# Where the low half of the feed-forward input lies in SBUF

## The chip, the cores and the metric

The kernel runs on one NeuronCore of a Trainium2 chip. The metric is the device time of one execution in microseconds (us). TensorE (PE) multiplies, VectorE (DVE) and ScalarE (ACT) work element by element, GpSimd (POOL) takes a few small roots, and SyncE (SP) issues the transfers. SBUF is the on-chip memory: an offset below is a byte offset within each of its 128 partitions. PSUM holds TensorE's results.

## The reference

Two transformer stacks run one after the other on 256 tokens of width 1024. The first has four layers; each is feed-forward, mixer, feed-forward, each with a norm before and after:

```python
def swiglu(x, w_in, w_out):
    gate, up = jnp.split(x @ w_in, 2, axis=-1)      # w_in 1024 x 5632
    return (jax.nn.silu(gate) * up) @ w_out          # w_out 2816 x 1024

for layer in range(4):
    h = h + 0.5 * rmsnorm(swiglu(rmsnorm(h, g[0]), ffn_w_in[layer, 0], ffn_w_out[layer, 0]), g[1])
    h = h + rmsnorm(mixer(rmsnorm(h, g[2])), g[3])   # sliding window, GLA, RWKV-7, sliding window
    h = h + 0.5 * rmsnorm(swiglu(rmsnorm(h, g[4]), ffn_w_in[layer, 1], ffn_w_out[layer, 1]), g[5])
```

The second stack has two layers (latent attention, neighbourhood attention) on latent and context tokens, each with a gated feed-forward block with a short convolution. Everything is float32.

## The kernel before

Every engine's instructions are written out by hand in one order for the whole program; nothing is scheduled later. Each engine waits on counting semaphores for named events.

TensorE multiplies in the format float32r, which keeps fewer bits than float32. So each operand is split in two: a high half, rounded to float32r (ScalarE, lines 708 and 886), and a low half, the rest (VectorE, lines 716 and 892). A product then takes three matmuls, issued by `mm3` on lines 186, 187 and 188: high by high, high by low, low by high. In this text a *triple* is one such group. Each matmul has its own load of 128 x 128 weights (the stationary side, PEld in the profile) and streams the other operand (256 or 512 columns).

There are feed-forward blocks numbered 0 to 8 and 10. Blocks 0 to 7 and 10 work on 256 tokens and get their memory from `ffn_memory`; block 8 works on 512 tokens (latent and context) and has memory of its own. In `pe_core`, a block of 256 tokens makes 22 steps, one for each 128 of the 2816 hidden columns. A step multiplies the input by 128 gate columns and 128 up columns: 2 x 8 triples, 48 matmuls of 256 columns, in which pieces of the weights are stationary and the input's halves `xh`, `xl` stream. Then it multiplies the hidden values of the step before by the output weights: four triples, 12 matmuls of 512 columns, in which the halves of the hidden values (`hs`) are stationary and pieces of the output weights stream. The first step has none of these 12, the last steps and the end of the block arrange them a little differently.

The input's halves are made once a block: `dve_gain` (line 699) writes the normed and transposed input to the buffer `xt`, `act_split_x` (line 708) rounds it into `xh`, and `dve_split_x` (line 716) writes `xl = xt - xh`. `xl` goes to the first half of `fast_xt`, which is the same memory as `xt` under the type float32r; so the subtraction is in place.

SBUF is laid out as follows. The long-lived buffers come first: the ring of six weight slots at offset 16,512, `xt`/`fast_xt` at 94,336, the constants (12,676 bytes, an odd length) at 131,200. The arena starts at 153,888 and is handed out anew for each phase; all its buffers of blocks 0 to 7 and 10 are called `a` in the profile. Their sizes are multiples of 1024 bytes. Divided by 64, the offsets of the ring and of `fast_xt` leave 0, and the offset of every arena buffer leaves 32. In a block of 256 tokens the six pairs of weight pieces lie at 153,888 to 203,040, `xh` at 203,040, an unused buffer of 8192 bytes at 211,232, and `ht` and `hs` behind it.

Other places of the program show other combinations, and they are used below. In block 8 both input halves and all pieces are in the arena. In the GLA projections `xh` is in the arena, `xl` in `fast_xt`, the high weights in the arena and the low weights in the ring. In the sliding-window output projection the weight pieces stream from the arena while the attention result is the stationary side, its high half in the arena and its low half in `fast_xt`. In neighbourhood attention the high halves are in the arena (called `r` there), the low ones in `fast_xt` and the ring.

Of the kernel before, what the change touches and what calls it, by code (L numbers as in the profile page):

```python
# [8 lines left out]
F32R = mybir.dt.float32r  # L9
# [5 lines left out]
T = 256  # L15
# [146 lines left out]
def v3(ap, b):  # L162
    return ap.rearrange("p (a b) -> p a b", b=b)
# [3770 lines left out]
def ffn_memory(K, f, w_in, w_out):  # L3934
    c = Core()
    c.w_in, c.w_out = w_in, w_out
    c.pieces = [(K.arena(1024, F32R), K.arena(1024, F32R)) for _ in range(6)]
    c.xs = v3(K.arena(2048, F32R), T), v3(K.fast_xt[:, 0:2048], T)
    K.arena(2048)
    c.ht = [K.arena(T) for _ in range(2)]  # L3940
    c.hs = [(K.arena(T, F32R), K.arena(T, F32R)) for _ in range(LATE)]
    c.gcol, c.row = None, lambda sp: None
    c.turn, c.next = range(6), None
    K.ffn[f], K.xs[f] = c, c.xs
    return c


def first_ffn(K, f):

    layer, second = f // 2, f % 2  # L3950
    c = ffn_memory(K, f, K.I["ffn_w_in"][layer, second], K.I["ffn_w_out"][layer, second])
    tag = ("f", f)
    n = 3 * layer + (2 if second else 0) + 1
    c.gcol = K.col("norm_g", n // 3 * 48 + n % 3 * 16, 8) if n < 12 else None
    c.row = lambda sp: load_row(K, sp, (tag, "g"), K.I["norm_g"][layer, 5 if second else 1], D, (K.s.dve, (tag, 1, "g1")))
    c.after = ("f", f - 1) if f else "setup"
    c.normed = ("f", f - 1) if f else "first"
    for t in range(2):
        K.sm[tag, t] = K.small(6)
# [10 lines left out]
def program(nc, I, out):  # L3970
    K = Core()
    K.nc, K.I = nc, I
    with ExitStack() as ctx:
# [78 lines left out]
        M_na = na_memory(K)  # L4052
        open_phase(K)
        ffn_memory(K, 10, I["ffn_w_in_2"][1], I["ffn_w_out_2"][1])
        M_conv = conv_memory(K, 10, 1, 0)
        for t in M_conv.tiles:
# [180 lines left out]
```

## Time and profile before

| | us |
|---|---|
| median of three runs (3408.6 to 3419.03) | 3408.88 |
| the profiled execution | 3408.6 |
| its span, from the first instruction to the last | 3406.8 |
| TensorE busy | 3239.8 |
| VectorE busy | 1961.1 |
| ScalarE busy | 1516.6 |
| mean granted TensorE clock, as a share of full speed | 0.983 |

The profile is of one execution. A matmul's duration in it is modelled at its end, and the next one starts before it is over; so the cost of a matmul in a dense stream is read from the distance between starts in the timeline, not from its duration. A timeline row gives the start in us with two decimals; over n matmuls the distance is known to about 10 ns / n.

### The profile page before, as it was taken

What the parts mean: (1) busy time and instruction counts of PE and PEld (TensorE: products, weight loads), DVE (VectorE), ACT (ScalarE), POOL (GpSimd) and SP (SyncE); (2) the same over time, 40 slices, a digit from 0 to 9 for tenths busy, and PEclk for the clock granted to TensorE, in tenths of its full rate; (3) what the DMA queues carried; (4) which work ended last, traced back from release to release, by engine and by line L of the source; (5) the groups of instructions that cost most, each with busy time, mean ns of one, the idle gap of its engine ahead of it and who ended that gap; (6) DMA issues with size and microseconds to landing.
All of it is one profiled execution on the core that took longest, in us unless ns stands there. A gap on an engine that the chain in (4) does not pass through costs nothing.

```text
span 3406.8 us, 49232 instructions
## 1 busy us (share of the span) xinstructions
PE 3239.8 (95%) x21142; PEld 2854.5 (84%) x21142; DVE 1961.1 (58%) x2964; ACT 1516.6 (45%) x2538; POOL 178.6 (5%) x201
## 2 busy tenths in 40 slices
PE   6998999999999999998999989999999999999898
PEld 6987998978898987696989978987878887887797
DVE  4557555557555555674555565555456555825777
ACT  4446444454445443213444455454544344524554
POOL 0000000003000000230000000000011000100100
PEclk9999999999999999998999999999999999999999
DMA  6563656555556544414556554551013333531452
GB/s 228 186 203 106 210 186 225 189 169 178 192 189 224 188 157 149 136 44 150 190 180 211 191 173 155 186 181 28 26 62 112 123 125 125 178 93 62 132 190 99
DMA packets 411239, 522.01 MB, mean 153 GB/s; under 512 B 41575, under 2 KB 353500, under 8 KB 410892
## 3 DMA queue, kind: packets, MB, share of 16 engines
q1 hardware_dynamic: 405980, 516.23, 46.1%
q8 instruction: 166, 2.72, 0.3%
q0 software_dynamic: 816, 2.10, 0.2%
q10 hardware_dynamic: 4224, 0.52, 0.1%
q14 instruction: 53, 0.43, 0.0%
HBM read 516.19 MB, written 2.10 MB: 152 GB/s over the span
## 4 chain that ended last, share of the span: by engine, by line
PE 86%; DVE 7%; ACT 4%; issue 1%; DMA 1%; POOL 0%; SPq 0%; DVEq 0%; ACTq 0%; POOLq 0%
PE ps L186 24%; PE ps L188 23%; PE ps L187 23%; PE ps L178 5%; PE ps L196 2%; PE ps L1226 2%; DVE fast_xt L716 1%; ACT a L1246 1%; DVE small L1283 1%; PE ps L559 1%; PE ps L1938 1%; PE ps L3802 0%; PE ps L3799 0%; DVE tmp L646 0%; DVE a L1279 0%
## 5 line engine op out<-in xcount | busy, mean ns | idle before, releaser
L186 PE MATMUL ps<-a 128*128 128x256 f32 (+1 forms) x4832 | 1519.1, 314 | 37.2 <-DVE fast_xt L716 15.9
L188 PE MATMUL ps<-a 128*128 128x256 f32 (+1 forms) x4664 | 1456.2, 312 | 0.0
L186 PEld LDWEIGHTS ps<-a 128*128 128x128 f32 x4832 | 914.9, 189 | 100.9 <-DVE fast_xt L716 15.3
L187 PE MATMUL ps<-fast_xt,a 128*128 128x256 f32 x3400 | 958.3, 282 | 0.0
L188 PEld LDWEIGHTS ps<-a 128*128 128x128 f32 x4664 | 887.1, 190 | 52.1
L892 DVE TENSOR_TENSOR a<-ring,a 128x1024 fp32r<-128x1024 f32 x594 | 693.5, 1221 | 348.5 <-ACT a L886 348.5
L886 ACT ACTIVATE a<-ring 128x1024 fp32r<-128x1024 f32 x594 | 586.4, 1049 | 232.3 <-PE ps L188 231.4
L187 PEld LDWEIGHTS ps<-fast_xt,a 128*128 128x128 f32 x3400 | 645.3, 190 | 7.4
L187 PE MATMUL ps<-a 128*128 128x512 f32 (+1 forms) x1368 | 527.3, 385 | 0.0
L187 PEld LDWEIGHTS ps<-a 128*128 128x128 f32 x1368 | 257.8, 188 | 43.3
L990 ACT ACTIVATE tmp<-ps 128x256 f32<-128x256 f32 x176 | 67.6, 384 | 487.0 <-PE ps L188 487.0
L996 DVE TENSOR_TENSOR a<-tmp,ps 128x256 f32<-128x256 f32 x176 | 74.1, 421 | 279.3 <-ACT tmp L990 279.3
L617 POOL TENSOR_TENSOR small<-small,cst 128x1 f32<-128x1 f32 (+1 forms) x78 | 59.4, 763 | 2774.8 <-DVE small L612 1940.2
L186 PE MATMUL ps<-r 128*128 128x512 f32 (+2 forms) x372 | 137.1, 369 | 5.5 <-DVE fast_ring L355 3.2
L958 DVE TENSOR_TENSOR a<-a 128x256 fp32r<-128x256 f32 x198 | 84.2, 425 | 96.0 <-ACT a L952 96.0
L187 PE MATMUL ps<-fast_ring,r 128*128 128x512 f32 (+1 forms) x336 | 128.7, 383 | 0.0
L952 ACT ACTIVATE a<-a 128x256 fp32r<-128x256 f32 x198 | 82.9, 419 | 96.5 <-DVE a L996 85.7
L1226 PE MATMUL ps<-a 128*128 128x64 f32 x832 | 109.1, 276 | 11.4 <-ACT a L1258 11.0
L1226 PEld LDWEIGHTS ps<-a 128*128 128x128 f32 x832 | 102.1, 194 | 19.3 <-ACT a L1258 17.4
L2731 DVE TENSOR_TENSOR a<-ring,a 128x1024 fp32r<-128x1024 f32 x88 | 105.6, 1222 | 20.6 <-ACT a L2725 19.2
L2725 ACT ACTIVATE a<-ring 128x1024 fp32r<-128x1024 f32 x88 | 90.3, 1051 | 12.0 <-PE ps L188 12.0
L1246 ACT ACTIVATE a<-a,small 128x128 f32<-128x128 f32 (+2 forms) x96 | 51.5, 537 | 98.8 <-DVE small L1288 98.7
(378 smaller groups left out, 3850.7 us busy)
## 6 DMA issues: line engine op xcount, KB each, us to landing
ring<-in_ffn_w_in_dram SPq DMA_DIRECT2D x220, 1024.0 KB, 7.5
ring<-in_ffn_w_out_dram SPq DMA_DIRECT2D x121, 1024.0 KB, 5.0
ring<-in_ada_w_dram SPq DMA_DIRECT2D x48, 1024.0 KB, 5.5
ring<-in_swa_w_qkv_dram SPq DMA_DIRECT2D x12, 1024.0 KB, 8.1
ring<-in_gla_w_in_dram SPq DMA_DIRECT2D x12, 1024.0 KB, 6.9
ring<-in_rwkv_w_rkv_dram SPq DMA_DIRECT2D x12, 1024.0 KB, 5.2
ring<-in_na_w_qkv_dram SPq DMA_DIRECT2D x12, 1024.0 KB, 5.2
ring<-in_swa_w_o_dram SPq DMA_DIRECT2D x8, 1024.0 KB, 5.5
```

Source lines behind the costliest of these rows:

```text
L178: ins = pe.x.matmul(out, l, r, start=start and i == 0, stop=stop and i == n - 1)
L186: pe.x.matmul(out, lh, rh, start=start and i == 0, stop=False)
L187: pe.x.matmul(out, lh, rl, start=False, stop=False)
L188: ins = pe.x.matmul(out, ll, rh, start=False, stop=stop and i == n - 1)
L886: act.x.activation(hi, raw, AF.Copy).then_inc(*K.s.act.up("hi", name, f, j))
L892: dve.x.tensor_tensor(lo, raw, hi.bitcast(F32), SUB).then_inc(*K.s.dve.up("lo", name, f, j))
L952: act.x.activation(K.ffn[f].hs[j % LATE][0], K.ffn[f].ht[j % 2], AF.Copy).then_inc(*s.act.up("hh", f, j))
L958: dve.x.tensor_tensor(hl, K.ffn[f].ht[j % 2], h.bitcast(F32), SUB).then_inc(*s.dve.up("hl", f, j))
L1226: ins = pe.x.matmul(bank[:, h * 64:(h + 1) * 64], A.PT[m % 3][:, tk(g * per + b)], values(u, g, b), start=b == 0, stop=b == per - 1)
L1246: ins = act.x.activation(A.P[i % 3][:, c], src[:, c], AF.Exp, scale=1.0 if A.masked else A.scale, bias=A.nm[u.job][:, h:h + 1], accum_out= ...
L2725: act.x.activation(hi, raw, AF.Copy).then_inc(*K.s.act.up("hi", name, 8, j))
L2731: dve.x.tensor_tensor(lo, raw, hi.bitcast(F32), SUB).then_inc(*K.s.dve.up("lo", name, 8, j))
```

## The change

The buffer for `xl` in blocks 0 to 7 and 10 is taken from the arena, at offset 211,232, where the unused 8192 bytes were; the first half of `fast_xt` is no longer used by these blocks. All other buffers keep their offsets.

```diff
@@ -3935,8 +3935,7 @@
     c = Core()
     c.w_in, c.w_out = w_in, w_out
     c.pieces = [(K.arena(1024, F32R), K.arena(1024, F32R)) for _ in range(6)]
-    c.xs = v3(K.arena(2048, F32R), T), v3(K.fast_xt[:, 0:2048], T)
-    K.arena(2048)
+    c.xs = [v3(K.arena(2048, F32R), T) for _ in range(2)]
     c.ht = [K.arena(T) for _ in range(2)]
     c.hs = [(K.arena(T, F32R), K.arena(T, F32R)) for _ in range(LATE)]
```

No instruction is added, removed or moved on any engine, and no wait is. What differs is one operand of one matmul in three. On TensorE, at the start of block 0 (`a14` is `xh`, `a2` and `a3` are a pair of weight pieces, `cst,hc` a transposition), the program had:

```order
L196 MATMUL ps<-cst,hc 128x128 [waits s_act]
L196 MATMUL ps<-cst,hc 128x128 x3
L186 MATMUL ps<-a14,a2 128x256 [waits s_dve]
L187 MATMUL ps<-fast_xt,a2 128x256
L188 MATMUL ps<-a14,a3 128x256
```

After the change the same place on TensorE reads (`a15` is the new `xl`):

```order
L196 MATMUL ps<-cst,hc 128x128 [waits s_act]
L196 MATMUL ps<-cst,hc 128x128 x3
L186 MATMUL ps<-a14,a2 128x256 [waits s_dve]
L187 MATMUL ps<-a15,a2 128x256
L188 MATMUL ps<-a14,a3 128x256
```

The middle matmul of every triple of 256 columns streams from `a15`; its place, its weights and its waits are as before. On VectorE, before block 0, the subtraction of line 716 writes elsewhere (`a6` to `a9` are weight pieces):

```order
 L824 TENSOR_SCALAR hc<-h,small 128x512
 L699 TENSOR_TENSOR xt<-ps,cols 128x4x128 x2
-L716 TENSOR_TENSOR fast_xt<-xt,a14 128x4x128 x4
+L716 TENSOR_TENSOR a15<-xt,a14 128x4x128 x4
 L892 TENSOR_TENSOR a7<-ring,a6 128x1024
 L892 TENSOR_TENSOR a9<-ring,a8 128x1024
```

It is no longer in place; its neighbours and their order stay.

## Rows read from the trace of the kernel before

**Rows 1.** The page, part 1: engine, busy us (share of the span), instructions.

```profile
PE 3239.8 (95%) x21142; PEld 2854.5 (84%) x21142; DVE 1961.1 (58%) x2964; ACT 1516.6 (45%) x2538; POOL 178.6 (5%) x201
```

**Rows 2.** The page, part 4: the chain that ended last, shares of the span.

```profile
PE ps L186 24%; PE ps L188 23%; PE ps L187 23%; PE ps L178 5%; PE ps L196 2%; PE ps L1226 2%; DVE fast_xt L716 1%; ACT a L1246 1%; DVE small L1283 1%; PE ps L559 1%; PE ps L1938 1%; PE ps L3802 0%; PE ps L3799 0%; DVE tmp L646 0%; DVE a L1279 0%
```

**Rows 3.** Stretch in block 2: from:to, length; busy PE, PEld, DVE, ACT, POOL; clock, DMA, GB/s.

```profile
549.00:717.00 168.00, 168.00 (x1207) 158.52 (x1206) 86.04 (x100) 73.63 (x99) 0.00 (x0) 1.00 0.62 201
```

**Rows 4.** Group by line and shape: count | busy us, mean ns | idle before.

```profile
L187 PE MATMUL ps<-fast_xt,a 128*128 128x256 f32 x3392 | 955.4, 282 | 0.0
```

**Rows 5.** Timeline, PE, one step of block 0: start us, us, engine, line, op, out<-in.

```profile
98.93 0.28 PE L186 MATMUL ps<-a 128*128 128x256 f32 x1
99.04 0.28 PE L187 MATMUL ps<-fast_xt,a 128*128 128x256 f32 x1
...
104.58 0.40 PE L186 MATMUL ps<-a 128*128 128x512 f32 x1
...
105.27 0.39 PE L186 MATMUL ps<-a 128*128 128x512 f32 x1
...
107.31 0.28 PE L186 MATMUL ps<-a 128*128 128x256 f32 x1
```

**Rows 6.** Stretches: that step, and one of block 8 with 256 columns; PE alone.

```profile
98.93:107.31 8.38, 8.38 (x61) 1.00 0.42 132
2586.91:2592.31 5.40, 5.40 (x48) 1.00 0.45 141
```

**Rows 7.** Timeline, PE, block 8: both halves of the input in the arena, 256 columns, then 512.

```profile
2586.91 0.28 PE L186 MATMUL ps<-a 128*128 128x256 f32 x1
2587.03 0.28 PE L187 MATMUL ps<-a 128*128 128x256 f32 x1
...
2592.31 0.40 PE L186 MATMUL ps<-a 128*128 128x512 f32 x1
...
2593.00 0.40 PE L186 MATMUL ps<-a 128*128 128x512 f32 x1
...
2595.05 0.39 PE L186 MATMUL ps<-a 128*128 128x512 f32 x1
```

**Rows 8.** Timeline, PE, GLA projections: input halves in a and fast_xt, weights in a and ring.

```profile
751.12 0.28 PE L186 MATMUL ps<-a 128*128 128x256 f32 x1
...
756.73 0.28 PE L186 MATMUL ps<-a 128*128 128x256 f32 x1
```

**Rows 9.** Timeline, PE, attention output: pieces stream, a and fast_xt are the stationary side.

```profile
2017.65 0.28 PE L186 MATMUL ps<-a 128*128 128x256 f32 x1
...
2020.14 0.28 PE L186 MATMUL ps<-a 128*128 128x256 f32 x1
```

**Rows 10.** Timeline, PE, 512 columns: block 8, all in the arena.

```profile
2595.28 0.39 PE L187 MATMUL ps<-a 128*128 128x512 f32 x1
...
2606.16 0.39 PE L187 MATMUL ps<-a 128*128 128x512 f32 x1
```

**Rows 11.** Timeline, PE, 512 columns: neighbourhood attention, halves in r and fast_xt.

```profile
2992.97 0.39 PE L186 MATMUL ps<-r 128*128 128x512 f32 x1
2993.20 0.39 PE L187 MATMUL ps<-fast_xt,r 128*128 128x512 f32 x1
...
2999.15 0.39 PE L186 MATMUL ps<-r 128*128 128x512 f32 x1
```

**Rows 12.** VectorE's subtraction of line 716: count: min/median/max ns, first and last start; who waited.

```profile
L716 DVE TENSOR_TENSOR fast_xt<-xt,a x48: 680/684/694, 31.1 to 3203.0; 128x512 fp32r<-128x512 f32 x48
  PE ps L186: 15.9, 9
```

## The prediction

> **What bounds the kernel now.** I read four views, from coarse to fine. The first part of the page shows TensorE busy 95% of the span, VectorE 58% and ScalarE 45% [rows 1]. The chain of waits says where the end comes from: lines 186, 187 and 188, the three matmuls of a triple, hold 24%, 23% and 23% of the span; the VectorE line that the change touches, 716, holds 1% [rows 2]. A stretch inside block 2 shows what a feed-forward block looks like: TensorE is busy 168.00 of 168.00 us at the full clock (1.00, the 2.4 GHz level), VectorE 86.04 and ScalarE 73.63 [rows 3]. So inside these blocks nothing but TensorE counts, and the other two have about half of the time free. Last the timeline, since in a dense stream a matmul's cost is the distance between starts. One step of block 0 runs from 98.93 to 107.31, 8.38 us [rows 5], with no idle time in it and the full clock [rows 6]. It falls in two: 48 matmuls of 256 columns from 98.93 to 104.58, 5.65 us or 117.7 ns each, and 12 of 512 columns to 107.31, 2.73 us or 227.5 ns each. All steps but the first and last of a block have this form; there are 22 in each of nine blocks, 198.
>
> 256 columns at 2.4 GHz are 106.7 ns and 512 are 213.3. So a matmul costs 11.0 ns more than its columns in the one stream and 14.2 in the other. That surplus is what this change can touch.
>
> **The change, part by part.**
>
> *The streamed operand.* In 22 x 8 x 2 = 352 matmuls of each of nine blocks, 3168 of the 3392 matmuls that the group of line 187 counts [rows 4], the streamed low half moves from `fast_xt` (offset leaves 0 when divided by 64) to the arena (leaves 32). Its two neighbours in the triple stream from the arena already. The order shows no other difference, so everything hangs on whether TensorE's spacing depends on where operands lie. The trace has matmuls of the same form with other placements, all at the full clock, and their spacing is not one number:
>
> - 256 columns, all four operands in the arena (block 8): 45 starts from 2586.91 to 2592.31, 5.40 us or 120.0 ns each; the rows stand 0.12 apart [rows 7], with no idle time in between and the clock at 1.00 [rows 6].
> - 256 columns, streamed halves mixed, weights all in the arena (the blocks in question): 117.7 ns [rows 5].
> - 256 columns, streamed halves mixed, weights mixed too (GLA): 48 starts from 751.12 to 756.73, 5.61 us or 116.9 ns [rows 8].
> - 256 columns, streamed halves all in the arena, weights mixed (attention output): 21 starts from 2017.65 to 2020.14, 2.49 us or 118.6 ns [rows 9].
> - 512 columns, all in the arena: 48 starts from 2595.28 to 2606.16, 10.88 us or 226.7 ns [rows 10]. 512 columns, mixed: 27 starts from 2992.97 to 2999.15, 6.18 us or 228.9 ns [rows 11].
>
> So placement does tell, by 2 to 3 ns a matmul. After the change the blocks have the placement of the first row of this list: both halves and all weight pieces in the arena. At 256 columns each step towards uniform placement costs: with mixed weights 118.6 - 116.9 = 1.7 ns, and the most alike pair, 120.0 - 117.7 = 2.3 ns. I take 120.0, since block 8 issues the same triples with the same kinds of buffers in the same arena. A step then pays 48 x 2.3 = 0.11 us more.
>
> *The 512-column part of a step.* Its own operands do not move, but its first triple follows the 256-column stream. Before, that triple takes 105.27 - 104.58 = 0.69 us, against 3 x 0.2267 = 0.68 in the settled stream, and the 12 take 2.73 us [rows 5]. In block 8, where a uniform 256-column stream goes before, the first triple takes 2593.00 - 2592.31 = 0.69 us and the 12 take 2595.05 - 2592.31 = 2.74 us [rows 7]. Settled throughout they would be 12 x 0.2267 = 2.72. So this term is between -0.01 and +0.01 us a step; I take +0.01, as block 8 has it.
>
> *VectorE's subtraction.* It is now out of place. There are 48 such instructions in the trace, four in each of the nine blocks and four in each of three mixers, 680 to 694 ns each, and TensorE waited for them 9 times, 15.9 us together [rows 12]. The time does not depend on anything I can see that the change alters: source and destination types, sizes and waits stay. Bounded from both sides by the spread of the row, -4 to +10 ns each, on the path 9 times: under 0.1 us. I take 0.
>
> *The freed `fast_xt`.* No transfer or write waited for it to come free, and the diff takes out no wait, so nothing can start earlier. 0.
>
> *The sum.* 198 steps x (0.11 + 0.01) = 23.8 us. Where TensorE runs at the lower clock the surplus may vanish; the mean granted clock is 0.983 of full speed over the whole span, so I take off 2%, 0.4 us. The profiled execution took 3408.6 us, 1.8 more than its span of 3406.8 and 0.3 less than the median of the runs, 3408.88. 3408.6 + 23.4 = 3432 us. The bounds of the main term: its reading is good to 0.01 us over 45 and 48 starts, 0.4 ns together, times 9504 matmuls is 4 us either way; with the other term, 3427 to 3435 if the mechanism holds.
>
> [...]
>
> **The rivals.**
>
> *No change.* The spacing of 120.0 ns may belong to something else in block 8: its halves lie 16,384 bytes apart instead of 8192, and its input is read with a stride of 2048 bytes from one k to the next instead of 1024. Then the blocks of 256 tokens keep 117.7 ns, and the time is 3408.6. For it: no third place has all operands in the arena at 256 columns. Against it: the other places differ in stride too and fall in line by placement alone, and a stride between instructions is not seen by any one instruction.
>
> *A part of it.* Only the difference of the mixed-weight rows is due to the stream, 1.7 ns, and the rest of the 2.3 is block 8's own. 9504 x 1.7 = 16 us: 3425.
>
> *The other side, faster.* At 512 columns the sign is reversed: uniform placement has 226.7 ns, mixed 228.9 [rows 10, 11]. If what counts is that a stream alternates between two placements (a switch costs, a repetition does not), the blocks gain 2.2 ns a matmul, 9504 x 2.2 = 21 us: 3388. It decides from the first triple on: starts 0.115 apart instead of 0.118. Against it stands the only uniform row at 256 columns, which is slower than the mixed ones.
>
> *More than forecast.* If the surplus of 13.3 ns also shows in the 512-column part as a lasting disturbance, at 231 ns as its first triple runs (0.69 over 3 is 230), the 12 cost 12 x 3.3 = 0.04 us a step more: another 8 us, 3440.
>
> *That the change doesn't do what it says* can be left out: the order shows the new operand in its place.
>
> **How the numbers follow.** 120.0 ns as in block 8: 0.74, 3432 (3427 to 3435). A part of it, 3425: 0.07. No change, 3408.6: 0.11. Faster, 3388: 0.05. More, 3440: 0.03. The range of 3418 to 3437 holds the first two, 0.81, and leaves out the rest; its low end is a little under the part case. A measurement of this kernel can tell about 0.3%, 10.2 us, from no change. Slower by more than that are the first, second and last case, 0.84, less 0.01 for a part so small that it drowns: 0.83. Within it: 0.12. Faster: 0.05.
>
> **What would show it.** In the timeline of a step: 48 starts of 256 columns 120 ns apart instead of 117.7, a step of 8.50 us instead of 8.38, in all nine blocks alike; the 12 of 512 columns 2.72 to 2.75 us. The busy times of VectorE and ScalarE and the waits for line 716 stay as they are. Block 8, the mixers and neighbourhood attention keep their spacing. If the steps are still 8.38 us long, the placement was not the cause of block 8's spacing. If they are 8.38 and the kernel is slower all the same, the time is between the blocks, where I expect nothing. If they are shorter, alternation was the cost.

## The result, and the profile after

The changed kernel takes 3443.45 us (median of 4 executions, 3441.36 to 3445.46; three more lie at 3444.57 to 3445.59), the kernel before in the same rounds 3408.99 (4 executions, 3408.6 to 3419.03). The ratio is 1.0096, with an interval of 1.0082 to 1.011. By the medians it is 34.5 us slower, where I had forecast 23.4. The time lies above the range. One execution in the slow state, 3513.33 us in experiment 1, is left out of every median, count and ratio below.

Part 1 of the page, in the columns of [rows 1]: TensorE is busy 34.5 us more than before, and VectorE, ScalarE and GpSimd stay within 1.2 us.

```profile
PE 3274.3 (95%) x21142; PEld 2885.6 (84%) x21142; DVE 1961.2 (57%) x2964; ACT 1516.9 (44%) x2538; POOL 177.4 (5%) x201
```

Part 4, the chain that ended last, answers to [rows 2]. The same three lines hold the span, and line 716 has less of it than before.

```profile
PE ps L186 24%; PE ps L187 24%; PE ps L188 23%; PE ps L178 5%; PE ps L196 3%; PE ps L1226 2%; PE ps L559 1%; PE ps L1938 1%; PE ps L3802 1%; PE ps L3799 1%; DVE small L1283 1%; ACT a L1246 1%; DVE a L716 0%; PE ps L3478 0%; DVE xt L699 0%
```

The groups of line 187 with 256 columns answer to [rows 4]: of the 3392 matmuls that streamed from `fast_xt`, 224 still do (the mixers), and 3168 have moved, as counted.

```profile
L187 PE MATMUL ps<-a 128*128 128x256 f32 x3232 | 921.1, 285 | 0.0
...
L187 PE MATMUL ps<-fast_xt,a 128*128 128x256 f32 x224 | 63.9, 285 | 0.0
```

The timeline of one step of block 0, on TensorE, answers to [rows 5].

```profile
100.55 0.28 PE L186 MATMUL ps<-a 128*128 128x256 f32 x1
100.67 0.28 PE L187 MATMUL ps<-a 128*128 128x256 f32 x1
...
106.31 0.40 PE L186 MATMUL ps<-a 128*128 128x512 f32 x1
...
107.00 0.40 PE L186 MATMUL ps<-a 128*128 128x512 f32 x1
...
109.05 0.28 PE L186 MATMUL ps<-a 128*128 128x256 f32 x1
```

The 48 matmuls of 256 columns now take 106.31 - 100.55 = 5.76 us, 120.0 ns each instead of 117.7; the 12 of 512 take 2.74; the step takes 8.50 us instead of 8.38. The trace keeps the starts to 1 ns, and by these the two parts are 5.752 and 2.748 us, where they were 5.650 and 2.730. The first two distances among the 48 are 114 and 119 ns, all that follow 120, give or take 1; before the change the distances ran through 114 to 121 ns in a pattern of nine. It is so in all nine blocks: of the 162 steps of this form in the middle of a block, 129 are 8.500 us and the others 8.499 or 8.501 (before, 161 were 8.380 and one 8.379). VectorE's subtraction (line 716) answers to [rows 12]: 36 of its 48 instructions write to the arena now, at the same 680 to 692 ns, and TensorE waited 13.9 us for them instead of 15.9.

```profile
L716 DVE TENSOR_TENSOR a<-xt,a x36: 680/683/692, 30.9 to 3235.4; 128x512 fp32r<-128x512 f32 x36
L716 DVE TENSOR_TENSOR fast_xt<-xt,a x12: 680/684/693, 230.7 to 2011.2; 128x512 fp32r<-128x512 f32 x12
...
  PE ps L186: 13.9, 9
```

So the steps are what was forecast, and something else costs 11 us. I split the span of both profiled executions at the steps. The 19 middle steps of each of the nine blocks (18 of the form above and one with only six matmuls of 512 columns, which went from 7.02 to 7.14 us) take 1420.7 us before and 1441.3 after, 20.5 more. The other three rows of 48 in each block make it about 23, an estimate at the full clock: 27 x 0.10 = 2.8 us. The whole rest went from 1986.1 to 2000.3. In that rest the two differ by the clock. Adding up TensorE's clock record, the kernel before has 116.3 us at the lower level (1.2 GHz), the changed one 142.3, and none of it lies in a middle step: it comes in the pauses before a block and its first steps, in the mixers and in the parts between the two stacks and at the end. (Both records run 2 us past the last instruction.) Two pauses show it. First two stretches of the kernel before (columns as in [rows 3]): the pause before block 4, from the last matmuls of block 3 on, and the pause before block 2. The clock is 1.00 in both.

```profile
1062.00:1090.00 28.00, 22.41 (x189) 18.01 (x188) 20.28 (x39) 17.34 (x34) 2.54 (x4) 1.00 0.49 161
524.00:548.00 24.00, 18.87 (x181) 15.64 (x180) 18.50 (x35) 14.86 (x28) 2.51 (x4) 1.00 0.49 160
```

In the changed kernel, TensorE alone, the stretch behind the pause before block 2 and the one behind the pause before block 4:

```profile
524.00:548.00 24.00, 19.18 (x150) 0.93 0.50 165
1090.00:1105.00 15.00, 12.17 (x78) 0.77 0.47 145
```

A mean of 0.93 over 24 us is 24 x 0.07 x 2 = 3.4 us at half speed, and 0.77 over 15 us is 15 x 0.23 x 2 = 6.9. Together 10.3 us of the 26; the rest came in other pauses, in both signs. If half of the time at the lower clock were lost, the 26 us would cost 13. In every profile taken of any of these kernels the span, less the middle steps, less half of the time at the lower clock, is 1921.5 to 1929.7 us (before 1927.9, after 1929.1), and the two differ by 20.5 + 1.2 + 13.0 = 34.7 = 3441.5 - 3406.8. But half is a ceiling, since TensorE also waits in these stretches. Experiment 5 shows it: the kernel before with eight more matmuls has 33.7 us more at the lower clock in its profile, and its rest, the delay taken off, is only 9.6 us longer. By the table of experiment 5 the 26 us cost about 9 (0.0038 of mean clock, at 2.3 us for each 0.001), an estimate. Some 3 of the other 5 us are the steps outside the middle; 2 to 3 us stay without a cause.

Two questions were open. Why do the steps cost 120.0 ns: is it what I read (all operands leaving the same when divided by 64), or another property of the place? And does the clock's part belong to the change, or to the two executions that I compared?

### The profile page after: what moved, and what is told of

It is laid out like the page before. It is cut to its first block, busy times and chain, and to the rows that moved or that the text cites. A ratio compares the mean times of both kernels' runs of the same rounds, so it can differ in the third digit from the quotient of the medians.

```text
span 3441.5 us, 49232 instructions
## 1 busy us (share of the span) xinstructions
PE 3274.3 (95%) x21142; PEld 2885.6 (84%) x21142; DVE 1961.2 (57%) x2964; ACT 1516.9 (44%) x2538; POOL 177.4 (5%) x201
## 4 chain that ended last, share of the span: by engine, by line
PE 87%; DVE 7%; ACT 4%; issue 1%; DMA 1%; POOL 0%; SPq 0%; DVEq 0%; ACTq 0%; POOLq 0%
PE ps L186 24%; PE ps L187 24%; PE ps L188 23%; PE ps L178 5%; PE ps L196 3%; PE ps L1226 2%; PE ps L559 1%; PE ps L1938 1%; PE ps L3802 1%; PE ps L3799 1%; DVE small L1283 1%; ACT a L1246 1%; DVE a L716 0%; PE ps L3478 0%; DVE xt L699 0%
## 5 line engine op out<-in xcount | busy, mean ns | idle before, releaser
L186 PE MATMUL ps<-a 128*128 128x256 f32 (+1 forms) x4832 | 1528.4, 316 | 35.5 <-DVE a L716 13.9
L188 PE MATMUL ps<-a 128*128 128x256 f32 (+1 forms) x4664 | 1466.6, 314 | 0.0
L187 PE MATMUL ps<-a 128*128 128x256 f32 (+1 forms) x4536 | 1432.1, 316 | 0.0
L186 PEld LDWEIGHTS ps<-a 128*128 128x128 f32 x4832 | 929.7, 192 | 101.5 <-DVE a L716 13.9
L188 PEld LDWEIGHTS ps<-a 128*128 128x128 f32 x4664 | 897.7, 192 | 52.8
L187 PEld LDWEIGHTS ps<-a 128*128 128x128 f32 x4536 | 873.4, 193 | 50.6
L886 ACT ACTIVATE a<-ring 128x1024 fp32r<-128x1024 f32 x594 | 585.7, 1047 | 234.6 <-PE ps L188 233.7
L1226 PEld LDWEIGHTS ps<-a 128*128 128x128 f32 x832 | 102.1, 194 | 19.3 <-ACT a L1258 17.5
L196 PE MATMUL ps<-cst,hc 128*128 128x128 f32 x256 | 42.8, 321 | 56.4 <-DVE hc L677 40.5
L2725 ACT ACTIVATE a<-ring 128x1024 fp32r<-128x1024 f32 x88 | 90.4, 1051 | 12.7 <-PE ps L188 12.0
L349 ACT ACTIVATE a<-ring 128x1024 fp32r<-128x1024 f32 x67 | 68.8, 1055 | 51.7 <-PE ps L188 51.4
```

Of the source, the lines that this page charges most:

```text
L186: pe.x.matmul(out, lh, rh, start=start and i == 0, stop=False)
L187: pe.x.matmul(out, lh, rl, start=False, stop=False)
L188: ins = pe.x.matmul(out, ll, rh, start=False, stop=stop and i == n - 1)
L196: ins = pe.x.transpose(bank[0:m, i * 128:i * 128 + p], b, K.ident[0:p, 0:p])
L886: act.x.activation(hi, raw, AF.Copy).then_inc(*K.s.act.up("hi", name, f, j))
L1226: ins = pe.x.matmul(bank[:, h * 64:(h + 1) * 64], A.PT[m % 3][:, tk(g * per + b)], values(u, g, b), start=b == 0, stop=b == per - 1)
```

## The experiments

Steps below are middle steps at the full clock. An offset of `xl` is counted from `xh` plus 8192 bytes, where the changed kernel has it; so it is the distance between the two halves, less a multiple of 256. In the kernel before it is 96 modulo 256: `fast_xt` lies 203,040 + 8192 - 94,336 = 116,896 bytes below that place, which is 457 x 256 - 96.

### 1. The whole arena moved by 32 bytes

```diff
# against the kernel before, among the constants ahead of the arena
+        sb("pad", 8)
```

> The kernel before, with 32 unused bytes ahead of the arena. xl stays in fast_xt, far from xh, but now the offset of every large buffer (ring, fast_xt, arena) is a multiple of 64. Theory A (what counts is whether the offsets of consecutive operands agree modulo 64): the steps of the nine blocks take 8.50 us as after the change, not 8.38, and the streams that were mixed elsewhere (GLA, neighbourhood attention) settle at 120.0 ns for 256 columns and 226.7 ns for 512. Theory B (what counts is that xl lies in another region of SBUF than xh): the steps stay at 8.38 us. By A the whole is some 20 us over the kernel before, less 2 to 13 us for about 1600 matmuls of 512 columns, give or take 10 us of time at the low clock between the blocks; by B it is at 3409 give or take the same 10.

3438.41 us (3 executions), ratio 1.0069 (1.0049 to 1.0089). One step of block 0 in the timeline:

```profile
115.98 0.28 PE L186 MATMUL ps<-a 128*128 128x256 f32 x1
...
121.63 0.39 PE L186 MATMUL ps<-a 128*128 128x512 f32 x1
...
124.39 0.28 PE L186 MATMUL ps<-a 128*128 128x256 f32 x1
```

8.41 us in all nine blocks, neither 8.50 nor 8.38. The 256-column part is 5.65 us, as before the change, although every operand now leaves 0 when divided by 64. So my reading "the same modulo 64" falls. In neighbourhood attention the 512 columns went to 231.1 ns from 228.9 instead of to 226.7, the GLA projections to 117.7 from 116.9: alike modulo 64 is not what makes them quick or slow. The place does count, down to 32 bytes. The whole is 23 us over the 3415.81 of the kernel before in the same rounds, near the 20 of theory A, but by luck: the steps give 198 x 0.033 = 7 us of it, and the three executions have a mean clock of 0.977 where the kernel before has 0.981.

### 2. and 3. The low half at another offset

```diff
# block:      0  1  2  3  4   5   6   7   10     x 4 bytes
+XL_OFF = {0: 0, 1: 2, 2: 4, 3: 6, 4: 8, 5: 10, 6: 12, 7: 14, 10: 16}
-    c.xs = [v3(K.arena(2048, F32R), T) for _ in range(2)]
+    o = XL_OFF[f]
+    c.xs = [v3(K.arena(2048, F32R), T), v3(K.arena(2048 + 16, F32R)[:, o:o + 2048], T)]
```

> The changed kernel, with xl in the arena in all nine blocks, but behind an offset that differs from block to block: 0, 8, 16, 24, 32, 40, 48 and 56 bytes in blocks 0 to 7 and 64 in block 10. Read is the length of a step in each block. Theory A (offsets modulo 64): 8.50 us in blocks 0 and 10, 8.38 in block 4 (32 bytes, the difference that the kernel before had), and something between or beside these in the others. Theory B (region): 8.50 us in all nine. A third, C (only whole 32-byte units count): 8.50 where the offset divides by 32 evenly in pairs, one other value for all the rest.

Steps of 8.54, 8.36, 8.45, 8.46 and 8.54 in turn, 8.56 and 8.42 in turn, 8.55, 8.46, 8.41 and 8.45 us, in the order of the blocks. Block 1, with 8 bytes:

```profile
427.00 0.28 PE L186 MATMUL ps<-a 128*128 128x256 f32 x1
...
432.55 0.40 PE L186 MATMUL ps<-a 128*128 128x512 f32 x1
...
435.36 0.28 PE L186 MATMUL ps<-a 128*128 128x256 f32 x1
```

48 matmuls in 5.55 us, 115.6 ns (by the starts in ns 5.558 and 115.8), quicker than anything before. But the 512-column part grew from 2.74 to 2.81: the spare 64 bytes had moved `ht` and `hs` as well. Block 0, whose `xl` has not moved at all, has 8.54 for 8.50. So this sweep changed two things at once, and no theory's table came out: A had 8.38 in block 4, B 8.50 everywhere. The next kernel has `xl` 32 bytes on in all blocks, with the same move of `ht` and `hs`:

```diff
+    c.xs = [v3(K.arena(2048, F32R), T), v3(K.arena(2048 + 16, F32R)[:, 8:8 + 2048], T)]
```

> The changed kernel, with xl in the arena and 32 bytes further on in all nine blocks. Theory A: steps of 8.38 us, and since then every stretch of the program has the timing of the kernel before, the clock falls at the same places too: 3409 us, ratio 1.000. Theory B: 8.50 us and 3443 us, ratio 1.0096. If the lost 12 us between the blocks belong to the placement in the arena as such and not to the timing, 3409 + 12 = 3421.

3443.11 us (4), ratio 1.0085 (1.007 to 1.01). Steps alternate between 8.56 and 8.42 us in every block, 8.49 on average, so the time is as with 8.50. Theory A's 8.38 us and 3409 are missed; theory B's 3443 is met, but experiment 4 rules B out, so this is luck too. Since two lengths alternate in steps of one block, in which `xl` stays where it is, what a step costs does not depend on `xl` alone; I take it that the buffers of `ht` and `hs`, which change from step to step, enter.

### 4. Is it the region, or the offset modulo something?

Here 1024 spare bytes keep `ht` and `hs` alike modulo 256.

```diff
# bytes: 0, 96, 352, 864, 128, 256, 512, 64 in blocks 0 to 7, 32 in block 10
+XL_OFF = {0: 0, 1: 24, 2: 88, 3: 216, 4: 32, 5: 64, 6: 128, 7: 16, 10: 8}
+    o = XL_OFF[f]
+    c.xs = [v3(K.arena(2048, F32R), T), v3(K.arena(2048 + 256, F32R)[:, o:o + 2048], T)]
```

> The changed kernel, with xl behind an offset that differs from block to block, and now with 1024 bytes of room for it, so that ht and hs behind it move by 1024 bytes and keep their place in any smaller unit. Offsets in bytes: 0, 96, 352, 864, 128, 256, 512 and 64 in blocks 0 to 7, 32 in block 10. The earlier sweep showed that 64 bytes are not neutral, so theory A in its first form (modulo 64) has fallen; A2 says modulo 128, and no other property of the place. A2: 8.50 us in blocks 0, 4, 5 and 6 (offsets that 128 divides), and 8.38 in blocks 1, 2 and 3, since 96, 352 and 864 leave 96 modulo 128, as fast_xt does against xh in the kernel before. If the period is 256 or 512 or 1024 bytes, only those of 352 and 864, or only 864, give 8.38. Theory B (another region of SBUF is what helps): none of the nine gives 8.38, since all lie in the arena.

Blocks 1 (96 bytes), 5 (256) and 7 (64):

```profile
427.58 0.28 PE L186 MATMUL ps<-a 128*128 128x256 f32 x1
...
433.23 0.40 PE L186 MATMUL ps<-a 128*128 128x512 f32 x1
...
435.96 0.28 PE L186 MATMUL ps<-a 128*128 128x256 f32 x1
...
1677.59 0.28 PE L186 MATMUL ps<-a 128*128 128x256 f32 x1
...
1683.34 0.40 PE L186 MATMUL ps<-a 128*128 128x512 f32 x1
...
1686.09 0.28 PE L186 MATMUL ps<-a 128*128 128x256 f32 x1
...
2188.96 0.28 PE L186 MATMUL ps<-a 128*128 128x256 f32 x1
...
2194.61 0.39 PE L186 MATMUL ps<-a 128*128 128x512 f32 x1
...
2197.37 0.28 PE L186 MATMUL ps<-a 128*128 128x256 f32 x1
```

| offset, bytes | 0 | 256 | 512 | 96 | 352 | 864 | 128 | 64 | 32 |
|---|---|---|---|---|---|---|---|---|---|
| modulo 256 | 0 | 0 | 0 | 96 | 96 | 96 | 128 | 64 | 32 |
| step, us | 8.50 | 8.50 | 8.50 | 8.38 | 8.38 | 8.38 | 8.37 | 8.41 | 8.38 |

This settles the main question. With `xl` in the arena, 96 bytes on, the step is the 8.38 us of the kernel before: the arena as a region costs nothing. The offset that block 0 of the changed kernel has repeats its 8.50 us at 256 and 512; the one of the kernel before repeats its 8.38 at 352 and 864; 128 is unlike 0. And 64 bytes gives the 8.41 of experiment 1, where the shift of the arena against `fast_xt` had left just 64. What counts is the offset of `xl` against the arena's other buffers modulo 256 bytes; the changed kernel put it on 0. I call it the distance of the halves, but no run tells `xh` from the weight pieces here: both leave the same when divided by 256, and neither was moved without the other. One execution took 3427.5 us.

### 5. Eight more matmuls in block 0: does a moved pause move the clock?

```diff
# after the wait for xl, in the core of a block; the results are overwritten
+            if f == 0 and j == 1 and n == 0:
+                for _ in range(8):
+                    pe.x.matmul(bank[:, 0:T], wh[:, 0, :], xh[:, 0, :], start=True, stop=True)
```

In the changed kernel:

> The changed kernel, with 8 extra matmuls of 256 columns at the start of the second step of block 0, whose result is overwritten: 0.96 us in the midst of a dense stream, and the same program after it. Two theories on the 12 us between the blocks. P (the clock falls and rises at moments that the pauses of the program meet differently when they are moved in time): the time at the low clock changes by several us from the 142 us of the changed kernel, in either direction, and the whole changes by something other than 1 us, by up to 10. S (the denser or slower streams as such bring the low clock): 142 us at the low clock give or take 7, and the whole at 3444 to 3445 us.

In the kernel before:

> The kernel before with 8 extra matmuls of 256 columns in the second step of block 0, 0.94 us. Theory P (the low clock falls where the pauses of the program happen to lie): steps of 8.38 us, span less the middle steps less half of the time at the low clock stays at 1928 us give or take 3 as in all profiles so far, and the mean clock of the executions moves within 0.978 to 0.983 together with the time. Theory S (the low clock comes with the steps of 8.50 us): the mean clock stays at 0.981 to 0.983 and the time within 2 us of the kernel before.

With 24 in the place of 8, about 3 us of delay, in the kernel before and in the changed one:

> As the kernel before with 8 extra matmuls, with 24 of them, 2.8 us. P: the mean clock is another one than with 8, the time follows it. S: mean clock 0.981 to 0.983, time 1 to 4 us over the kernel before.

> The changed kernel with 24 extra matmuls in the second step of block 0, 2.9 us. P: in some shift the changed kernel should meet a mean clock of 0.981 or more too, and then be 24 to 26 us over the kernel before at the same clock instead of 34. S: mean clock 0.978 to 0.980, 3444 to 3449 us.

| | us (executions) | ratio to the kernel before | at the lower clock, us |
|---|---|---|---|
| changed, 8 more | 3445.43 (4) | 1.0089 (1.0074 to 1.0104) | 149.7 |
| before, 8 more | 3415.54 (12) | 1.0002 (0.9994 to 1.001) | 150.0 |
| before, 24 more | 3421.04 (10) | 1.0017 (1.0005 to 1.0029) | 142.8 |
| changed, 24 more | 3443.84 (4) | 1.0088 (1.0068 to 1.0108) | 149.3 |

The kernel before with 1 us of delay has 34 us more at the lower clock in its profiled execution than without, yet in the median it is as fast: the profile of one execution shows one draw of the clock. The steps of the changed kernel stay 8.50.

Neither theory came through. P wanted the changed kernel to meet a mean clock of 0.981 in some shift: it has 0.979 in the mean with 8 more and with 24 more, as S said (0.976 to 0.980). S wanted the kernel before to keep 0.981 to 0.983 with 24 more: it fell to 0.979 in the mean, and the time rose by 6 us where the delay is 2.8. P's constant of 1928 us give or take 3 was missed with 8 more, at 1921.5, which is the sign that half of the time at the lower clock is too much to take off.

The rounds of all experiments gave 52 executions of the kernel before, on four chips with means of 3413.4 to 3416.7 us. Its mean clock runs from 0.977 to 0.985, its time from 3407 to 3427 us; the mean is 3415.0 at 0.981. The execution on which I built the sum, with 0.983 and 3408.6 us, is one of the best. By equal mean clock:

| mean clock | kernel before, us (executions) | changed kernel, us (executions) | difference |
|---|---|---|---|
| 0.978 | 3423.0 (2) | 3445.4 (5) | 22.4 |
| 0.979 | 3419.5 (10) | 3444.6 (3) | 25.1 |
| 0.980 | 3416.9 (5) | 3442.0 (3) | 25.1 |
| 0.982 | 3413.2 (12) | none | |
| 0.983 | 3411.7 (10) | none | |
| 0.984 | 3409.4 (4) | none | |

Not listed are one execution at 0.977, seven at 0.981 and one at 0.985, all of the kernel before.

The last column is the change without the clock: 22 to 25 us, for 23.4 forecast. The mean clock is known to 0.001, which is 2.3 us. On one chip in the same rounds (experiment 11) the differences are 24.6 us at 0.979 and 25.0 at 0.980.

### 6. Delays in blocks 1 and 3 of the changed kernel

The pauses with more time at the lower clock stand behind blocks 1 and 3, so the same 8 matmuls were put there (`if f in (1, 3) ...`).

> The changed kernel with 8 extra matmuls, 0.96 us, in the second step of block 1 and of block 3. In all three profiles with steps of 8.50 us (none, 8 or 24 extra matmuls in block 0) the clock falls for 3.4 us in the pause between blocks 1 and 2 and for 6.9 us about the one between blocks 3 and 4, and in none of the three with steps of 8.38 us; elsewhere the profiles differ among themselves. P, in the form that the place of a pause counts from the last change of the clock before it, which lies at the start of the same block: the shift of 1 us inside the block changes these two numbers, to 0 if it is enough, and the mean clock rises from 0.979. S: 3.4 and 6.9 us stay, the mean clock stays at 0.979, and the time is 3445 to 3446 us.

3447.54 us (6), ratio 1.0091 (1.0073 to 1.0109). Three stretches, TensorE alone: the pause between blocks 5 and 6, the one before block 2, and the one before block 4.

```profile
1800.00:1825.00 25.00, 20.59 (x174) 0.86 0.53 178
524.00:548.00 24.00, 18.41 (x154) 1.00 0.46 153
1090.00:1105.00 15.00, 11.36 (x96) 1.00 0.49 160
```

And the first stretch in the changed kernel:

```profile
1800.00:1825.00 25.00, 19.94 (x169) 1.00 0.69 232
```

The last two of the three stretches are at 1.00, where the changed kernel has 0.93 and 0.77: with a delay of 1 us the 3.4 and the 6.9 us are gone in the one profile taken, as P said. The mean clock did not rise, though P had it rise (0.979 over six executions). And the first stretch is at 0.86 now, where the changed kernel has 1.00, and the sum over the span is 166.4 us, the highest of all. So it seems that which pauses fall to the lower clock hangs on when they come, and that a change that moves them all reshuffles them. Repairing two by hand gains nothing.

### 7. and 8. Finer offsets

`ht` and `hs` alike modulo 256 again; 4, 8, 12, 16, 20, 24, 28 bytes in blocks 0 to 6, 48 in block 7, 160 in block 10, and then 36, 40, 44, 56, 60, 84, 92, 124 and 156.

```diff
+XL_OFF = {0: 1, 1: 2, 2: 3, 3: 4, 4: 5, 5: 6, 6: 7, 7: 12, 10: 40}           # experiment 7
+XL_OFF = {0: 9, 1: 10, 2: 11, 3: 14, 4: 15, 5: 21, 6: 23, 7: 31, 10: 39}     # experiment 8
```

> The changed kernel with xl at 4, 8, 12, 16, 20, 24 and 28 bytes beyond its place in blocks 0 to 6, 48 and 7 blocks' last, and 160 in block 10 (block 7 has 48), with 1024 bytes of room so that nothing behind it changes its place in any smaller unit. The last sweep has shown that 0, 256 and 512 give 8.50 us, 32 and 96 give 8.38, 128 gives 8.373 and 64 gives 8.413: by theory A3 the spacing is a function of the distance of xl and xh modulo 256. It must then repeat in the part of 256 columns what the first sweep had there: 8 bytes 5.56 us in 48 matmuls, 16 bytes 5.65, 24 bytes 5.66 or 5.75, 48 bytes 5.67, with 2.73 to 2.75 us for the 12 of 512 columns in place of 2.80. So the step with 8 bytes is 8.29 us, the shortest seen. If the spacing depends on more than this distance (on ht and hs, which lay 64 bytes further in the first sweep), these numbers do not come back.

> The same sweep as the last, with 36, 40, 44, 56, 60, 84, 92, 124 and 156 bytes in blocks 0 to 7 and 10. Nothing so far is below 8.287 us; 28 + 32, 28 + 64 and 28 + 128, which are 60, 92 and 156, would be as short if a unit of 32 bytes were all that counts; if not, they scatter between 8.37 and 8.50 like the rest.

| offset, bytes | 4 | 8 | 12 | 16 | 20 | 24 | 28 | 36 | 40 | 44 | 48 | 56 | 60 | 84 | 92 | 124 | 156 | 160 |
|---|---|---|---|---|---|---|---|---|---|---|---|---|---|---|---|---|---|---|
| step, us | 8.38 | 8.50 | 8.45 | 8.38 | 8.43 | 8.49 | 8.29 | 8.49 | 8.51 | 8.41 | 8.42 | 8.39 | 8.35 | 8.47 | 8.41 | 8.32 | 8.37 | 8.43 |

One execution each, 3432.5 and 3430.79 us. The step changes with almost every 4 bytes, by up to 0.2 us, and I found no rule: no unit of 32 or 64, no slope. At 8, 24, 36 and 40 bytes it is as long as at 0. At 8 bytes it is 8.50 here, where the 256-column part of experiment 2 was quickest; so the forecast of 8.29 fell, and with it the theory that the distance of the halves alone sets the spacing: the place of `ht` and `hs` changes what is best for `xl`. The best offset was 28, 8.287 us; 60, 92 and 156, which are 32, 64 and 128 further, are not as short.

### 9. and 10. Two versions for speed

Here the spare room is 256 bytes, so `ht` and `hs` stay alike modulo 256.

```diff
-    c.xs = [v3(K.arena(2048, F32R), T) for _ in range(2)]
+    c.xs = [v3(K.arena(2048, F32R), T), v3(K.arena(2048 + 64, F32R)[:, 2:2050], T)]   # 8 bytes
+    c.xs = [v3(K.arena(2048, F32R), T), v3(K.arena(2048 + 64, F32R)[:, 7:2055], T)]   # 28 bytes
```

> The changed kernel with xl 8 bytes beyond its place in all nine blocks. By A3 a step is 8.29 us, 0.09 less than before the change and 0.21 less than after: 198 x 0.09 = 18 us less than the kernel before in the dense stretches, 3397 us at the same mean clock, ratio 0.995. By the reading that only uniform against mixed counts: 8.38 us and 3415. On the clock: by theory S (slower steps bring more time at the low clock) its mean clock is 0.982 or more; by theory P (it is a matter of where the pauses fall) it may be anything from 0.978 to 0.984.

3444.99 us (6), ratio 1.0077 (1.0057 to 1.0097), steps of 8.50 us. I had taken the quick 256-column part of experiment 2 for `xl`'s own; experiment 7 shows that it was not. A miss.

> The changed kernel with xl 28 bytes beyond its place in all nine blocks, the offset whose block had the shortest step in the last sweep (8.287 us; the other eight had 8.38 to 8.50). If the step is set by the distance of xl and xh and by the way in which the stream is entered, and both are alike in all blocks, all nine have 8.287 us: 198 x 0.093 = 18 us less than the kernel before in the dense stretches, and at the same mean clock 3397 us where the kernel before has 3415. If it was peculiar to block 6, some blocks keep 8.4 to 8.5, and the time is between. The clock between the blocks adds or takes up to 8 us either way.

3398.73 us (3396.81 to 3406.04, 6 executions) against 3412.94 for the kernel before in the same rounds (11): ratio 0.996 (0.9945 to 0.9975). It beats both kernels. A step of block 0 in its timeline, and part 1 of its page:

```profile
115.11 0.28 PE L186 MATMUL ps<-a 128*128 128x256 f32 x1
...
120.67 0.40 PE L186 MATMUL ps<-a 128*128 128x512 f32 x1
...
123.40 0.28 PE L186 MATMUL ps<-a 128*128 128x256 f32 x1
```

```profile
PE 3228.4 (95%) x21142; PEld 2842.9 (84%) x21142; DVE 1961.7 (58%) x2964; ACT 1516.8 (45%) x2538; POOL 178.5 (5%) x201
```

The 48 take 5.56 us, 115.8 ns each, in all nine blocks. TensorE is busy 46 us less than in the changed kernel, with the same instructions in the same order; 198 x (8.50 - 8.287) = 42 of them are the steps. Against the kernel before the steps give 198 x 0.093 = 18.4 us. At a mean clock of 0.979, which this kernel has (mean of its six 3400.0), the kernel before takes 3419.5: 19.5 less.

### 11. The changed kernel once more

No edit, to have its clock beside more executions of the kernel before.

> The changed kernel itself, timed beside the kernel before in more rounds. By the account so far (24 us in the dense stretches, and the rest a matter of the clock between the blocks, which moves by itself from execution to execution), it is 24 to 26 us over the kernel before wherever two executions have the same mean clock, and the medians are 24 to 34 us apart. Had the change a third cost, executions of the same mean clock would be 34 us apart.

3444.49 us (4), ratio 1.0089 (1.0074 to 1.0104) to 3412.94; steps of 8.50, 143.0 us at the lower clock. The stretch before block 4, TensorE alone, has the same lapse as in the first profile, so this part is a property of the kernel and not only a draw. Indeed, by the two clock records the thirteen lapses from 540 to 2125 us are the same in place (1 us apart) and in length, 89 us in all; the two profiles differ before and behind them.

```profile
1090.00:1105.00 15.00, 13.14 (x86) 0.77 0.45 150
```

## Why the prediction was wrong in its number, and how far its mechanism held

**The place of an operand changes TensorE's spacing: right.** 120.0 ns and steps of 8.50 us, as read from block 8 [rows 7], in all nine blocks. The Trainium skill ("TensorE: Matmul & The Clock Gate", section "Back-to-back issue gap") gives the gap of an isolated warm matmul as columns over 2.4 plus 2.5 ns, with no term for an address. These runs have no isolated matmul to hold against it, but in their dense streams such a term is needed: 23 offsets gave steps from 8.29 to 8.51 us with the same instructions. The rival "No change" is out; "A part of it" (3425, 1.7 ns) falls with the 120.0 ns; experiment 4 shows more sharply that 120.0 ns was not block 8's own.

**Why: wrong.** "After the change the blocks have the placement of the first row of this list: both halves and all weight pieces in the arena" reads the cause as all operands leaving the same when divided by 64. Experiment 1 has that for all of them at 0 and takes 8.41. What the changed kernel and block 8 share is that the two streamed halves lie a multiple of 256 bytes apart (8192 and 16,384). The rows I had could not tell the two apart. That I took 120.0 from block 8 was right by luck: it has the offset that counts, for a reason that I had not read.

**The 512-column part: right to 0.01 us.** The rows give 2.74 us, the +0.01 taken; by the starts in ns it is +0.018, and the 256-column part +0.102 where +0.11 was taken, so that the two small errors cancel in the step. The rivals "More than forecast" through this part and "faster" through alternation are out: the part grew by 0.018 us and not by 0.04 to 0.05, and the uniform stream is the slower one at 256 columns.

**VectorE's subtraction and the freed buffer: right, 0.** 680 to 692 ns as before; the waits fell by 2.0 us.

**The surplus in the sum: right.** 198 x 0.12 - 0.4 = 23.4 us; measured at equal mean clock 22.4, 25.1 and 25.1, in the two profiles 20.5 for the middle steps and about 23 for all.

**The step that failed: "the time is between the blocks, where I expect nothing."** I gave that term 0, and took off 0.4 us for the lower clock as though its time stayed as it was. Measured it is some 11 of 34.5 us, in two parts. The changed kernel's mean clock in 11 executions is 0.0024 below that of the 52 of the kernel before; by the slope of the table in experiment 5 (3423.0 at 0.978 to 3409.4 at 0.984, 2.3 us for each 0.001) this is some 5 us. The rest, 5 to 6 us, is the base: the sum stands on 3408.6, and the median of the first four executions is 3408.99, while the kernel before has a mean of 3415.0 in 52. The mean of the changed kernel's 11 executions, 3444.3, is 29.3 us above 3415.0; even by that the time would have been 3408.6 + 29.3 = 3438, just over the top of the range, which I had built from the bounds of the steps alone. A term of ±5 us for the clock, readable in nothing but the spread of the three times shown (3408.6 to 3419.03), was left out.

**What stays open.** Why the changed kernel's mean clock is lower. The idea that slower steps bring it about does not hold: the version with 28 bytes has the shortest steps and a mean clock of 0.979 as well. That pauses which come at other times fall otherwise fits experiment 6, but is not shown by it, and which fall was not forecast by anything. Open too is the rule by which an offset modulo 256 gives a spacing, whether it is counted from `xh` or from the weight pieces, and how `ht` and `hs` enter it.

## What to carry to other kernels

Where TensorE is busy without a gap, the distance in SBUF between operands of consecutive matmuls, modulo 256 bytes, is a parameter worth 1.3% here (3398.73 against 3444.49 us). A multiple of 256 between two buffers that stream in turn, which power-of-two sizes handed out in a row give, was among the slowest offsets, but 8, 24, 36 and 40 bytes were as slow. So there is nothing to do but try: a few spare bytes, another number in each block, reading the steps' lengths in one profile. And when the base of a forecast is one execution, look at the spread of the times first: what lies in pauses at the lower clock can be redrawn by a change that moves them, and belongs into the range.

## What the runs showed of the hardware

- The spacing of matmuls of 256 columns at the full clock went from 115.8 to 120.0 ns in whole blocks by the streamed low half's offset alone, in steps as small as 4 bytes. The step repeats with 256 bytes (0, 256 and 512: 8.50 us; 96, 352 and 864: 8.38), and at offsets 64 and 96 it was the same with `xl` in `fast_xt` and in the arena.
- With `ht` and `hs` 64 bytes further the 12 matmuls of 512 columns went from 2.74 to as much as 2.81 us, and steps of one block alternated between 8.56 and 8.42 us.
- The lower clock never came in a block's middle steps, where TensorE is busy without a gap; it came 3.4 to 17 us at a time, mostly just after TensorE had waited. Not always: at 1355.7 us of the changed kernel, in a mixer, it fell after 20 us without a wait. With eight extra matmuls in blocks 1 and 3 the lapses in the pauses behind them were gone, and one of 6.8 us appeared before block 6.
- A microsecond at the lower clock cost about a third of a microsecond, an estimate: 0.001 of mean clock is 6.8 us at the lower clock, and goes with 2.3 us.
- The same kernel took 3407 to 3427 us over 52 executions, in step with its mean clock of 0.985 to 0.977.
